# A wide first matmul for 79 of the 128 expert "up" slabs, with the sum of its two halves on VectorE

## The chip, the cores and the metric

The kernel runs on one core of a Trainium2 chip. The metric is the device time of one launch in microseconds (us). The engines named are TensorE (PE, with its weight loads as PEld), VectorE (DVE), ScalarE (ACT), GpSimd (POOL) and SyncE (SP), which here only issues DMAs.

## The reference

A block of a language model runs over 256 tokens of width 1024, all in float32: a mixer (state space and short convolution), PEER (a feed-forward part with 16,384 experts of one neuron each), and then linear attention (HGRN2), a gated FFN, windowed attention and a second gated FFN. The change is in PEER and in two orders of linear attention:

```python
def peer_ffn(n, w_q, sub_keys, expert_u, expert_v):
    q = (t @ w_q).reshape(T, PEER_HEADS, 2, PEER_HALF)
    s = jnp.einsum('thsd,hskd->thsk', q, sub_keys)
    v_half, i_half = lax.top_k(s, PEER_TOPK)                  # 16 best of 128 keys, twice per head
    cand = v_half[:, :, 0, :, None] + v_half[:, :, 1, None, :]
    best, pos = lax.top_k(cand.reshape(...), PEER_TOPK)       # 16 best of the 256 sums
    experts = i1 * PEER_KEYS + i2
    gates = jax.nn.softmax(best)
    act = gelu(x . u[experts]) * gates                        # 128 of the 16384 experts per token
    return sum(act * v[experts])
...
    q, f, i, g = jnp.split(x @ w_in, 4)                       # linear attention (HGRN2)
    o = hgrn2_chunked(q, k, i, logf)
    return (rms_norm(o, out_norm) * silu(g)) @ w_out
```

## The kernel before

All weights pass as 524 slabs of 128x1024 float32, each by one DMA into a ring of four places (`raw`). TensorE multiplies float32 through the faster f32r format, and keeps the accuracy by splitting each operand in a high part and the rest: `split_hi` (ACT, L237, `whi`) and `split_lo` (DVE, L245, `wlo`) do this for a slab, `xhi` and `xlo` hold the two parts of the input x. A product is `whi*xhi + whi*xlo + wlo*xhi`.

PEER computes all 16,384 hidden values: 128 "up" slabs (numbered 0 to 127 here, N_U in the code), each giving one 128x256 tile, then 128 "down" slabs. An up slab by `up` (L273 to L275) is 8 x 3 matmuls of 256 columns, all summed in the first half of one PSUM bank; two banks take turns. ACT then takes the tile out with a Gelu straight from the bank (L1634), and counts it in the semaphore `up_evac`, on which TensorE waits before it writes that bank again: slab k+2 can't begin before the tile of slab k is out. A slab's place in `whi` is free for `split_hi` of slab k+4 when TensorE is through with slab k. SP stores the tile in memory.

Meanwhile DVE finds the experts: sorting work for each head, laid between the `split_lo` of slabs 0 to 62 by a planner (`plan`). It walks the slabs at 2.85 us each, charges 1.25 us for a split that DVE makes itself (POOL makes that of every other slab up to slab 47's step), and fills each step k with units ("half", "pairs", "places", "one_hots", "picked", "numbers") while they fit. In step k DVE makes the low split of slab k+3, then the units of step k. When all is known, six transposes stand in front of slab 59 (COLS_AT), and beside slabs 63 to 126 (E1 = 63, 64 steps) the gates are scattered to a table: in each step DVE makes one-hot rows for four tokens (`one_token`, L1847) and one tile for four (`four_tokens`, L1853), TensorE multiplies them in two pairs, one in the middle of the slab and one after it (L1591), and ACT takes the result out (L1664).

The gated FFNs already use another form, `up_halves` (L294, L298): `xhi` and `xlo` stand side by side in `x2`, so that one matmul of 512 columns takes both with the same weights `whi`, its result filling both halves of a bank, and `wlo*xhi` is added to the second half. That is 8 matmuls of 512 and 8 of 256 columns. It waits for the low split only in its middle. The two halves of the bank must then be added: ACT copies the one (L2523), DVE adds the other from the bank (L2574).

Linear attention runs 16 such `up` slabs over four banks, then 16 slabs by `up_wide` (L334 to L336), which writes four banks in the order 0, 1, 2, 3, the first of which has to wait until each bank is emptied of the earlier slabs. At its end, DVE makes split 15 and then `y(0)`, the low part of the first input (L2433) of the first output slab.

Of the kernel before, what the change touches and what calls it, by code (L numbers as in the profile page):

```python
# [131 lines left out]
def build(nc, t):  # L132
    ctx = ExitStack()
    with ctx:
# [185 lines left out]
        def up_wide(pe, n0, k, bank_free=None, banks_out=None):  # L320
# [4 lines left out]
            for tt in range(TT):  # L325
                x = slice(k * SEQ + tt * P, k * SEQ + (tt + 1) * P)
                for nh in range(2):
                    if bank_free is not None:
                        pe.wait_ge(bank_free, 2 * tt + nh + 1)
                    if banks_out is not None:  # L330
                        pe.wait_ge(up_evac, banks_out[2 * tt + nh])
                    o = bank[2 * tt + nh][:, :]
                    w = slice(q * 1024 + nh * 512, q * 1024 + (nh + 1) * 512)
                    nc.tensor.matmul(o, xhi[:, x], whi[:, w], start=k == 0, stop=False)  # L334
                    nc.tensor.matmul(o, xhi[:, x], wlo[:, w], start=False, stop=False)  # L335
                    last = nc.tensor.matmul(o, xlo[:, x], whi[:, w], start=False, stop=k == KT - 1)  # L336
# [1164 lines left out]
        def plan():  # L1501
# [11 lines left out]
            for k in range(E1):  # L1513
# [5 lines left out]
                spent = max(spent, 2.85 * (k - 1)) + (0.0 if k in by_pool else 1.25)  # L1519
# [27 lines left out]
        def pe_peer(pe):  # L1547
# [19 lines left out]
            up(pe, N_U, U_U, 0, 0, 4, SEQ, x_ready=lo_base(T_WQ, 1))  # L1567
            steps(pe, COLS_AT - 1, 4, lambda i, r: up(pe, N_U + 1, U_U + 1, i, r, 4, SEQ))
# [35 lines left out]
        def act_peer(act, chain):  # L1604
# [36 lines left out]
            steps(act, E1 - 12, 4, step1)  # L1641
            for k in range(E1 - 12, COLS_AT):
# [1467 lines left out]
```

## Time and profile before

| | us |
|---|---|
| median of 3 runs | 1676.4 (1676.38 to 1676.55) |
| profiled execution, its own time | 1676.54 |
| its span, first to last instruction | 1674.8 |
| TensorE busy | 1657.1 (99%) |
| DVE busy | 1309.1 (78%) |
| ACT busy | 1024.4 (61%) |
| granted TensorE clock, mean | 0.998 |

The span is the time between the first and the last instruction of the profile; 1.7 us of the execution lie around it. "Busy" of TensorE counts overlapping matmuls, so the pace of a slab is read from the starts of its instructions.

### The profile page before, as it was taken

Reading aid. Unit: us, or ns where it says so; the run is one execution under the profiler, and the core shown is the slowest. Engines: PE = TensorE matmul, PEld = TensorE weight load, DVE = VectorE, ACT = ScalarE, POOL = GpSimd, SP = SyncE. Lnnn points to the kernel's source line nnn. Section 1 sums busy time; section 2 is a strip of 40 time slices with the busy share of each in tenths; the row PEclk is TensorE's granted clock in tenths of the full one; section 3 lists DMA queues with packets and bytes.
Section 4 is the critical chain, followed back from the end, with each engine's and each line's share of the span. In section 5 each row is a group of like instructions: output and inputs, shape, how many; then the busy total and the mean of one; then the engine's idle time right before and its main releaser. Section 6 shows DMA issues by size and latency. Waiting matters only on the chain.

```text
span 1674.8 us, 34396 instructions
## 1 busy us (share of the span) xinstructions
PE 1657.1 (99%) x10855; PEld 1499.6 (90%) x10855; DVE 1309.1 (78%) x2404; ACT 1024.4 (61%) x1620; POOL 135.5 (8%) x121
## 2 busy tenths in 40 slices
PE   8999999999999999999999999999999999999998
PEld 7999899999999999988888888999888888888886
DVE  7867865899877777777777777899777778978776
ACT  7757555767556666655454554765566557766555
POOL 0035200444000000000000000210000000000000
PEclk9999999999999999999999999999999999999999
DMA  6543464777755555477777877542455554346553
GB/s 214 174 151 104 150 226 143 234 228 226 236 189 173 175 175 177 153 249 241 241 248 252 254 246 243 194 152 88 151 166 196 190 189 155 102 162 197 190 191 113
DMA packets 113614, 315.65 MB, mean 188 GB/s; under 512 B 12832, under 2 KB 44832, under 8 KB 113296
## 3 DMA queue, kind: packets, MB, share of 16 engines
q1 hardware_dynamic: 112032, 310.43, 57.4%
q0 software_dynamic: 1200, 4.07, 0.8%
q8 instruction: 37, 0.61, 0.1%
q10 hardware_dynamic: 320, 0.34, 0.1%
q14 instruction: 25, 0.20, 0.0%
HBM read 296.43 MB, written 18.35 MB: 188 GB/s over the span
## 4 chain that ended last, share of the span: by engine, by line
PE 94%; DVE 3%; ACT 2%; issue 1%; DMA 0%; ACTq 0%; DVEq 0%
PE bank L273 12%; PE bank L274 12%; PE bank L275 12%; PE bank L342 11%; PE bank L343 11%; PE bank L344 11%; PE bank L294 9%; PE bank L298 4%; PE bank L1591 3%; PE bank L2085 2%; PE bank L334 1%; PE bank L336 1%; PE bank L335 1%; DVE wlo L245 1%; PE bank L1287 1%
## 5 line engine op out<-in xcount | busy, mean ns | idle before, releaser
L245 DVE TENSOR_TENSOR wlo<-raw,whi 128x1024 fp32r<-128x1024 f32 x499 | 615.4, 1235 | 120.0 <-ACT whi L237 114.0
L237 ACT ACTIVATE whi<-raw 128x1024 fp32r<-128x1024 f32 x524 | 550.5, 1052 | 19.4 <-PE bank L336 11.4
L273 PE MATMUL bank<-x,whi 128*128 128x256 f32 (+3 forms) x1712 | 499.7, 292 | 0.7 <-DVE x L723 0.3
L275 PE MATMUL bank<-x,wlo 128*128 128x256 f32 (+3 forms) x1712 | 484.2, 283 | 0.0
L274 PE MATMUL bank<-x,whi 128*128 128x256 f32 (+3 forms) x1712 | 483.9, 283 | 0.0
L273 PEld LDWEIGHTS bank<-x,whi 128*128 128x128 f32 x1712 | 326.2, 191 | 3.9 <-issue 1.8
L274 PEld LDWEIGHTS bank<-x,whi 128*128 128x128 f32 x1712 | 326.8, 191 | 0.3
L275 PEld LDWEIGHTS bank<-x,wlo 128*128 128x128 f32 x1712 | 326.1, 190 | 0.0
L342 PE MATMUL bank<-whi,yhi 128*128 128x512 f32 x816 | 319.4, 391 | 1.2 <-DVE ylo L2433 1.1
L343 PE MATMUL bank<-wlo,yhi 128*128 128x512 f32 x816 | 318.1, 390 | 0.0
L344 PE MATMUL bank<-whi,ylo 128*128 128x512 f32 x816 | 317.6, 389 | 0.0
L342 PEld LDWEIGHTS bank<-whi,yhi 128*128 128x128 f32 x816 | 153.3, 188 | 33.1 <-DVE wlo L245 1.3
L344 PEld LDWEIGHTS bank<-whi,ylo 128*128 128x128 f32 x816 | 153.2, 188 | 32.5
L343 PEld LDWEIGHTS bank<-wlo,yhi 128*128 128x128 f32 x816 | 153.4, 188 | 29.7
L294 PE MATMUL bank<-x,whi 128*128 128x512 f32 x704 | 177.6, 392 | 0.8 <-DVE arena L2598 0.7
L1683 ACT ACTIVATE yhi<-h 128x256 fp32r<-128x256 f32 x128 | 53.5, 418 | 170.2 <-PE bank L344 169.6
L294 PEld LDWEIGHTS bank<-x,whi 128*128 128x128 f32 x704 | 129.2, 188 | 27.1 <-DVE arena L2598 1.1
L1634 ACT ACTIVATE h<-bank 128x256 f32<-128x256 f32 x128 | 49.2, 384 | 148.8 <-PE bank L275 148.6
L1892 DVE TENSOR_TENSOR ylo<-h,yhi 128x256 fp32r<-128x256 f32 x128 | 54.5, 425 | 68.2 <-ACT yhi L1683 68.0
L298 PEld LDWEIGHTS bank<-x,wlo 128*128 128x128 f32 x704 | 96.7, 190 | 6.7
L298 PE MATMUL bank<-x,wlo 128*128 128x256 f32 x704 | 100.3, 283 | 0.0
L1847 DVE TENSOR_SCALAR h<-iota,h 128x128 f32<-128x128 f32 x256 | 77.0, 344 | 21.7 <-PE bank L1591 21.7
(354 smaller groups left out, 1777.0 us busy)
## 6 DMA issues: line engine op xcount, KB each, us to landing
raw<-in_stream SPq DMA_DIRECT2D x524, 512.0 KB, 3.6
act_spill<-h SPq DMA_DIRECT2D x124, 128.0 KB, 3.3
h<-act_spill SPq DMA_DIRECT2D x124, 128.0 KB, 3.7
h<-in_x SPq DMA_DIRECT2D x2, 512.0 KB, 5.0
arena<-in_keys POOLq DMA_DIRECT2D x1, 1024.0 KB, 5.9
h_spill<-h SPq DMA_DIRECT2D x1, 1024.0 KB, 6.2
arena<-h_spill POOLq DMA_DIRECT2D x8, 128.0 KB, 3.7
arena<-in_g_final POOLq DMA_DIRECT2D x4, 128.0 KB, 3.7
```

Source lines behind the costliest of these rows:

```text
L237: nc.scalar.activation(whi[:, q * 1024:(q + 1) * 1024], raw[:, q * 1024:(q + 1) * 1024], ACT.Copy).then_inc(hi_ready, 1)
L245: nc.vector.tensor_tensor(wlo[:, q * 1024:(q + 1) * 1024], raw[:, q * 1024:(q + 1) * 1024], whi[:, q * 1024:(q + 1) * 1024].bitcast(F32), ...
L273: nc.tensor.matmul(bank[b][:, 0:T], whi[:, w], xhi[:, x], start=k == 0, stop=False)
L274: nc.tensor.matmul(bank[b][:, 0:T], whi[:, w], xlo[:, x], start=False, stop=False)
L275: last = nc.tensor.matmul(bank[b][:, 0:T], wlo[:, w], xhi[:, x], start=False, stop=k == KT - 1)
L294: return nc.tensor.matmul(bank[b][:, :], whi[:, w], both, start=k == 0, stop=k == KT - 1)
L298: return nc.tensor.matmul(bank[b][:, SEQ:2 * SEQ], wlo[:, w], xhi[:, k * SEQ:(k + 1) * SEQ], start=False, stop=stop, skip_group_check=True)
L342: nc.tensor.matmul(o, yhi[:, y], whi[:, w], start=first, stop=False, skip_group_check=True)
L343: nc.tensor.matmul(o, yhi[:, y], wlo[:, w], start=False, stop=False, skip_group_check=True)
L344: return nc.tensor.matmul(o, ylo[:, y], whi[:, w], start=False, stop=True, skip_group_check=True)
L1847: nc.vector.tensor_scalar(HOT1[:, y % 2 * P:(y % 2 + 1) * P], iota[:, :], c1(I1T), c1(GT_COLS), ALU.is_equal, ALU.mult).then_inc(s("hot_a" ...
L1892: nc.vector.tensor_tensor(ylo[:, yq * SEQ:(yq + 1) * SEQ], PRD[:, yq * SEQ:(yq + 1) * SEQ], yhi[:, yq * SEQ:(yq + 1) * SEQ].bitcast(F32), ...
```

## The change

In PEER, slabs 48 to 126 (H0 = E1 - 15 = 48; 15 slabs ahead of the scatter and the 64 beside it) are multiplied by `up_halves`; slab 127 stays with `up`. ACT, which had one Gelu from the bank, now has a copy of the second half of the bank (`half_out`) and a Gelu in place for the slab before (`half_gelu`). DVE gets one addition per slab (`half_sum`), which alone frees the bank. The planner charges 0.45 us for it. In the scatter loop DVE's low split comes one step later than it did. Stores and reads of the tiles wait for new semaphores. In linear attention the first wide slab takes the banks in the order in which they come free, and `y(0)` stands ahead of split 15. The keys' DMA counts in another semaphore.

```diff
-            for tt in range(TT):
+            for b in sorted(range(4), key=lambda b: banks_out[b] if banks_out else b):
+                tt, nh = b // 2, b % 2
...
+        H0 = E1 - 15
...
-                spent = max(spent, 2.85 * (k - 1)) + (0.0 if k in by_pool else 1.25)
+                spent = max(spent, 2.85 * (k - 1)) + (0.0 if k in by_pool else 1.25) + (0.45 if k > H0 else 0.0)
...
-            steps(pe, COLS_AT - 1, 4, lambda i, r: up(pe, N_U + 1, U_U + 1, i, r, 4, SEQ))
+            if H0:
+                steps(pe, H0 - 1, 4, lambda i, r: up(pe, N_U + 1, U_U + 1, i, r, 4, SEQ))
+            k1 = max(H0, 1)
+            steps(pe, COLS_AT - k1, 4, lambda i, r: up_halves(pe, N_U + k1, U_U + k1, i, r, 4))
...
-                up(pe, N_U + E1, U_U + E1, i, r, 4, SEQ, between=lambda: pair(i, r, 0))
+                up_halves(pe, N_U + E1, U_U + E1, i, r, 4, between=lambda: pair(i, r, 0))
                 pair(i, r, 1)
...
+            def half_out(k0, i, r):
+                q = (k0 + r) % 4
+                act.wait_ge(slabs_done, at(N_U + k0, i, r, 4) + 1 + RING)
+                act.wait_ge(spill_sem(q), rounds(k0, i, r, 4) * 16 + 16)
+                nc.scalar.activation(HR[:, q * SEQ:(q + 1) * SEQ], bank[(U_U + k0 + r) % 2][:, SEQ:2 * SEQ], ACT.Copy)\
+                    .then_inc(s("u_half"), 1)
...
+            def half_gelu(k0, i, r):
+                q = slice((k0 + r) % 4 * SEQ, ((k0 + r) % 4 + 1) * SEQ)
+                act.wait_ge(up_evac, at(U_U + k0, i, r, 4) + 1 + 2)
+                nc.scalar.activation(HR[:, q], HR[:, q], ACT.Gelu).then_inc(s("u_act"), 1)
...
+            def step_halves(k):
+                split_hi(act, N_U + k + AHEAD, 0, 0, 4)
+                half_out(k, 0, 0)
+                if k > H0:
+                    half_gelu(k - 1, 0, 0)
...
+            def half_sum(k0, i, r):
+                q = slice((k0 + r) % 4 * SEQ, ((k0 + r) % 4 + 1) * SEQ)
+                dve.wait_ge(s("u_half"), at(k0 - H0, i, r, 4) + 1)
+                nc.vector.tensor_tensor(HR[:, q], HR[:, q], bank[(U_U + k0 + r) % 2][:, 0:SEQ], ALU.add)\
+                    .then_inc(up_evac, 1)
...
                     split_lo(dve, N_U + k + AHEAD, 0, 0, 4)
+                if k > H0:
+                    half_sum(k - 1, 0, 0)
                 for kind, tt, arg in UNITS_AT[k]:
                     unit(kind, tt, arg)
...
+            def step(k0, i, r):
+                one_token(k0, i, r, 0)
+                one_token(k0, i, r, 1)
+                if k0:
+                    split_lo(dve, N_U + E1 + k0 - 1 + AHEAD, i, r, 4)
+                half_sum(E1 + k0 - 1, i, r)
+                one_token(k0, i, r, 2)
+                one_token(k0, i, r, 3)
+                four_tokens(k0 + 1, i, r)
...
             normed(1, 1)
+            y(0)
             split(15)
-            y(0)
             gated(1)
```

On VectorE, around steps 48 to 50 of PEER, the order before was this (L245 is a low split; L1793 is the last unit of step 48, L1748 to L1754 are "places" in step 49, L1766 and L1775 "one_hots" and "picked" in step 50):

```order
L1793 TENSOR_TENSOR arena<-arena 128x256 [waits dve_self]
L245 TENSOR_TENSOR wlo<-raw,whi 128x1024 [waits hi_ready]
L1748 TENSOR_SCALAR arena<-arena 128x128
L1749 TENSOR_SCALAR arena<-arena 128x128
L1751 CAST arena<-arena 128x256 [waits dve_self]
L1754 CAST arena<-arena 128x256 [waits dve_self]
L245 TENSOR_TENSOR wlo<-raw,whi 128x1024 [waits hi_ready,dve_self]
L1766 TENSOR_TENSOR arena<-arena 128x2048
L1775 TENSOR_TENSOR arena<-arena 128x2048 [waits dve_self]
L245 TENSOR_TENSOR wlo<-raw,whi 128x1024 [waits hi_ready,dve_self]
```

and it is now this (L1868 is `half_sum`, the first one that of slab 48):

```order
L1826 TENSOR_TENSOR arena<-arena 128x256 [waits dve_self]
L245 TENSOR_TENSOR wlo<-raw,whi 128x1024 [waits hi_ready]
L1868 TENSOR_TENSOR h<-h,bank1 128x256 [waits u_half]
L1781 TENSOR_SCALAR arena<-arena 128x128
L1782 TENSOR_SCALAR arena<-arena 128x128
L1784 CAST arena<-arena 128x256 [waits dve_self]
L1787 CAST arena<-arena 128x256 [waits dve_self]
L245 TENSOR_TENSOR wlo<-raw,whi 128x1024 [waits hi_ready,dve_self]
L1868 TENSOR_TENSOR h<-h,bank0 128x256 [waits u_half]
L1799 TENSOR_TENSOR arena<-arena 128x2048
L245 TENSOR_TENSOR wlo<-raw,whi 128x1024 [waits hi_ready,dve_self]
L1868 TENSOR_TENSOR h<-h,bank1 128x256 [waits u_half]
```

The sum of slab k stands in step k+1 behind the low split of slab k+4 and behind all units of step k. "picked" has moved a step on; later "numbers" moves from step 52 to 53, the next "one_hots" from 52 to 54 and "picked" from 53 to 55, where it stands with the last "numbers" and the gates.

On ScalarE, steps 49 and 50 were three lines, a high split, a Gelu from the bank and a high split (L1634):

```order
L237 ACTIVATE whi<-raw 128x1024 [waits slabs_done,raw_ready1]
L1634 ACTIVATE h<-bank0 128x256 [waits act_moved1,slabs_done]
L237 ACTIVATE whi<-raw 128x1024 [waits slabs_done,raw_ready2]
L1634 ACTIVATE h<-bank1 128x256 [waits act_moved2,slabs_done]
L237 ACTIVATE whi<-raw 128x1024 [waits slabs_done,raw_ready3]
```

and now the Gelu of the slab before (L1656), which waits for the sum on DVE through `up_evac`, stands between the copy (L1649) and the next high split:

```order
L237 ACTIVATE whi<-raw 128x1024 [waits slabs_done,raw_ready1]
L1649 ACTIVATE h<-bank0 128x256 [waits act_moved1,slabs_done]
L1656 ACTIVATE h<-h 128x256 [waits up_evac]
L237 ACTIVATE whi<-raw 128x1024 [waits slabs_done,raw_ready2]
L1649 ACTIVATE h<-bank1 128x256 [waits act_moved2,slabs_done]
L1656 ACTIVATE h<-h 128x256 [waits up_evac]
```

On TensorE, in a step of the scatter, the first pair of one-hot products (L1598, before L1591) now follows eight matmuls of 512 columns:

```order
L294 MATMUL bank0<-x2,whi 128x512 [waits up_evac]
L294 MATMUL bank0<-x2,whi 128x512 x7
L1593 ISA
L1595 REGISTER_ALU [waits hot_a]
L1598 MATMUL bank2<-ylo,h 128x128 [waits g_evac,hot_b]
L1593 REGISTER_ALU
L1598 MATMUL bank2<-ylo,h 128x128 [waits hot_a]
L298 MATMUL bank0<-x2,wlo 128x256 [waits lo_ready]
L298 MATMUL bank0<-x2,wlo 128x256 x7
```

It stood behind twelve of 256 columns, and the low split was waited for at the start of the slab; the wait for `lo_ready` now stands in the middle.

## Rows read from the trace of the kernel before

**Rows 1.** The page, busy time by engine (us, share, instructions).
```profile
PE 1657.1 (99%) x10855; PEld 1499.6 (90%) x10855; DVE 1309.1 (78%) x2404; ACT 1024.4 (61%) x1620; POOL 135.5 (8%) x121
```
**Rows 2.** Timeline ahead of the scatter: start us, length us, engine, line, operation [idle before].
```profile
427.49 0.38 ACT L1634 ACTIVATE h<-bank 128x256 f32<-128x256 f32 x1 [1.55 <-PE bank L275]
427.77 1.05 ACT L237 ACTIVATE whi<-raw 128x1024 fp32r<-128x1024 f32 x1
...
453.21 0.82 PE L1575 MATMUL bank<-ident,arena 128*128 128x128 f32 x6
```
**Rows 3.** Chain of waits, one gated FFN step: start us, us, what.
```profile
1238.02 1.81 PE bank L294 x8
1239.83 0.95 PE bank L298 x8
1240.79 1.84 PE bank L294 x8
```
**Rows 4.** Timeline, first and last of 128 groups of one-hot products.
```profile
466.82 0.61 PE L1591 MATMUL bank<-ylo,h 128*128 128x128 f32 x4
...
705.58 0.61 PE L1591 MATMUL bank<-yhi,h 128*128 128x128 f32 x4
```
**Rows 5.** Timeline of POOL and DVE at steps 47 to 49.
```profile
422.20 2.53 POOL L253 TENSOR_TENSOR wlo<-raw,whi 128x1024 fp32r<-128x1024 f32 x1 [3.87 <-DVE wlo L245]
...
429.00 1.22 DVE L245 TENSOR_TENSOR wlo<-raw,whi 128x1024 fp32r<-128x1024 f32 x1
430.14 0.22 DVE L1748 TENSOR_SCALAR arena<-arena 128x128 uint32<-128x128 uint32 x1
```
**Rows 6.** Groups by form: busy us, mean ns, idle before. The FFN's sum from a bank.
```profile
L2574 DVE TENSOR_TENSOR arena<-arena,bank 128x256 f32<-128x256 f32 x44 | 18.5, 420 | 18.0 <-ACT arena L2523 18.0
```
**Rows 7.** Timeline at the first output slab of linear attention.
```profile
1187.52 1.22 DVE L245 TENSOR_TENSOR wlo<-raw,whi 128x1024 fp32r<-128x1024 f32 x1
1187.75 0.47 ACT L2234 ACTIVATE yhi<-bank,arena 128x256 fp32r<-128x256 f32 x1 [0.62 <-PE bank L2135]
...
1188.65 0.48 DVE L2433 SCALAR_TENSOR_TENSOR ylo<-bank,arena,yhi 128x256 fp32r<-128x256 f32 x1
...
1189.28 0.47 PE L342 MATMUL bank<-whi,yhi 128*128 128x512 f32 x1 [1.13 <-DVE ylo L2433]
```
**Rows 8.** Timeline of units on DVE, and of ACT's exponentials, steps 50 to 53.
```profile
432.55 1.22 DVE L1766 TENSOR_TENSOR arena<-arena 128x2048 bf16<-128x2048 bf16 x1
...
436.53 1.28 ACT L1645 ACT_TABLE_LOAD   x1
...
437.34 1.47 DVE L1783 TENSOR_TENSOR arena<-arena 128x1024 bf16<-128x1024 bf16 x3
```
**Rows 9.** Waits between 421 and 466 us: us in total, times, longest.
```profile
DVE wlo L245 <- ACT whi L237: 7.8, 5, 2.3
```
**Rows 10.** Waits between 466 and 706 us, the scatter.
```profile
DVE wlo L245 <- ACT whi L237: 29.7, 64, 0.6
DVE h L1847 <- PE bank L1591: 21.7, 62, 0.4
```
**Rows 11.** Timeline, first wide slab to the second level, and one window (columns: rows 12).
```profile
1106.93 0.47 PE L334 MATMUL bank<-whi,x 128*128 128x512 f32 x1 [0.56 <-ACT arena L2190]
...
1122.09 1.31 DVE L2369 COPY arena<-bank 128x512 f32<-128x512 f32 x2
...
1123.54 3.81 PE L2085 MATMUL bank<-arena 128*128 128x128 f32 x32
...
1113.00:1120.00 7.00, 7.00 (x52) 6.48 (x51) 7.00 (x9) 4.87 (x6) 0.00 (x0) 1.00 0.65 178
```
**Rows 12.** Timeline and windows (PE, PEld, DVE, ACT, POOL busy, clock, DMA), start and end.
```profile
5.18 4.85 PE L835 MATMUL bank<-yhi 128*128 128x512 bf16 x11 [5.18 <-DMA h<-in_x]
...
1666.38 0.39 PE L344 MATMUL bank<-whi,ylo 128*128 128x512 f32 x1
...
1668.80:1669.00 0.20, 0.00 (x0) 0.00 (x0) 0.20 (x2) 0.00 (x0) 0.00 (x0) 0.88 0.00 0
```

More of the change, by code:

```diff
@@ L324, in up_wide @@
             pe.wait_ge(lo_ready, n0 + k + 1)
-            for tt in range(TT):
+            for b in sorted(range(4), key=lambda b: banks_out[b] if banks_out else b):
+                tt, nh = b // 2, b % 2
                 x = slice(k * SEQ + tt * P, k * SEQ + (tt + 1) * P)
[L327 to L336, printed above, removed]
+                if bank_free is not None:
+                    pe.wait_ge(bank_free, b + 1)
+                if banks_out is not None:
+                    pe.wait_ge(up_evac, banks_out[b])
+                o = bank[b][:, :]
+                w = slice(q * 1024 + nh * 512, q * 1024 + (nh + 1) * 512)
+                nc.tensor.matmul(o, xhi[:, x], whi[:, w], start=k == 0, stop=False)
+                nc.tensor.matmul(o, xhi[:, x], wlo[:, w], start=False, stop=False)
+                last = nc.tensor.matmul(o, xlo[:, x], whi[:, w], start=False, stop=k == KT - 1)
             last.then_inc(slabs_done, 1)
@@ L1639, in step1 @@
                 gelu(N_U, U_U, i, r)
-            steps(act, E1 - 12, 4, step1)
-            for k in range(E1 - 12, COLS_AT):
+            def step_halves(k):
[3 more added lines that the diff above has]
+                    half_gelu(k - 1, 0, 0)
+            steps(act, min(H0, E1 - 12), 4, step1)
+            for k in range(min(H0, E1 - 12), COLS_AT):
                 if k == E1 - 10:
@@ L1667, in act_peer @@
             split_hi(act, N_U + E1 + AHEAD, 0, 0, 4)
-            gelu(N_U + E1, U_U + E1, 0, 0)
+            half_out(E1, 0, 0)
+            half_gelu(E1 - 1, 0, 0)
             def step2(i, r):
@@ L1842, in dve_peer, with one_token @@
                     columns()
-            def one_token(i, r, y):
-                n = i * (4 * TPS) + r * TPS + y
+            def one_token(k0, i, r, y):
+                n = i * (4 * TPS) + (k0 + r) * TPS + y
                 dve.wait_ge(s("hot_free"), n - 2 + 1 + TPS)
@@ L1919, in pool_peer @@
             pool.wait_ge(y_lo, 16)
-            pool.dma_start(KEY, t["keys"]).then_inc(s("keys_in"), 16)
+            pool.dma_start(KEY, t["keys"]).then_inc(s("tri"), 16)
             for a in range(TOPK):
@@ L1956, in act_dram, with store @@
                     t["act_spill"][bass.ds(k, 1)].rearrange("a p c -> (a p) c")
-            def put(i, r):
-                sp.wait_ge(up_evac, at(U_U, i, r, 4) + 1 + 2)
-                sp.dma_start(act_dram(i, r), HR[:, r * SEQ:(r + 1) * SEQ]).then_inc(spill_sem(r), 16)
-            def store(i, r):
-                load(sp, N_U + lead, i, r, 4)
-                put(i, r)
-            steps(sp, KEYS - 2 * KEPT, 4, store)
-            for r in range(KEPT):
-                store(KEYS // 4 - 2, r)
+            def store(k0, i, r):
+                load(sp, N_U + lead + k0, i, r, 4)
+                if k0 < H0:
+                    sp.wait_ge(up_evac, at(U_U + k0, i, r, 4) + 1 + 2)
+                else:
+                    sp.wait_ge(s("u_act"), at(k0 - H0, i, r, 4) + 1)
+                q = (k0 + r) % 4
+                sp.dma_start(act_dram(i, r, k0), HR[:, q * SEQ:(q + 1) * SEQ]).then_inc(spill_sem(q), 16)
+            if H0:
+                steps(sp, H0, 4, lambda i, r: store(0, i, r))
+            steps(sp, KEYS - 2 * KEPT - H0, 4, lambda i, r: store(H0, i, r))
+            for k in range(KEYS - 2 * KEPT, KEYS - KEPT):
+                store(k, 0, 0)
             for k in range(KEYS - KEPT, KEYS):
```

43 lines of the change are left out of this document (24 added, 19 removed).

## The prediction

> **What bounds the kernel now.** I read the page's busy times first: TensorE is busy 1657.1 of 1674.8 us, 99% [rows 1]. So time is won by a shorter stream of matmuls alone, and any wait put in front of TensorE is lost in full. Next the timeline ahead of the scatter, for the pace of a slab: the Gelu of slab 49 starts at 427.49 and starts 0.25 us after the slab's last issue slot, so slab 49 ends at 427.24; the transposes behind slab 58 start at 453.21 [rows 2]. That is 25.97 us for 9 slabs, 2.88 us each, without a gap. The wide form is seen in the FFN: 1.81 + 0.95 us, the next slab starting 2.77 us after the first [rows 3]. In the scatter, group 1 of the one-hot products starts at 466.82 and group 128 at 705.58 [rows 4]: 127 halves in 238.76 us, 3.76 us for a step, of which 2.88 are the slab and 0.88 the two pairs. The first group stands 12 matmuls of 0.12 us into slab 63, which therefore begins at 465.4.
>
> **What the wide matmul gives.** 2.88 - 2.77 = 0.11 us per slab, 64 x 0.11 = 7.0 us in the scatter and 15 x 0.11 = 1.6 us ahead of it. The columns are the same (24 x 256 = 8 x 512 + 8 x 256); what goes is the fixed part of eight matmuls, 0.0135 us each. The Trainium skill speaks against this gain (TensorE: Matmul & The Clock Gate, "Wait — 56ns, not 53.3ns?"): a back-to-back matmul costs N/2.4 GHz plus about 2.5 ns. By that, as an estimate from the page, eight matmuls fewer are worth 0.02 us, and all 79 slabs 1.6 us. The rows show five times that per matmul, and I go by the rows.
>
> **The stretch ahead of the scatter.** Here the change adds a wait, and DVE is late for it. The bank of slab k, which slab k+2 needs, was freed by ACT's Gelu right behind slab k. It is now freed by DVE's sum, which stands in step k+1, behind all units of step k and behind a low split. DVE's low split of step 49 starts at 429.00, because step 48 waited for POOL's split (422.20 + 2.53 = 424.73) and then had a "pairs" unit [rows 5]. Nothing in those steps has changed. The low split holds DVE 1.14 us (430.14 - 429.00) [rows 5], and the sum takes 0.42, as the FFN's does [rows 6]: bank free at 430.56. How TensorE restarts from a DVE wait is seen in the first output slab of linear attention: 0.15 us after the 0.48 us that start at 1188.65, with a first matmul 0.08 longer than the usual 0.39 [rows 7], so 0.23 us. Slab 50 would start at 430.8. Its two predecessors in the wide form end at 427.02 (427.24 - 2 x 0.11). TensorE waits **3.8 us** there; before, DVE's lag cost nothing, since only slab 52 needed that low split.
>
> From there DVE, ACT and TensorE run in a ring. After slab k: 0.25 until ACT's copy, 0.28 to issue the next (427.49 to 427.77 [rows 2]), 0.30 for the Gelu of slab k-1, 1.05 for the high split [rows 2], 0.04 hop, 1.14 low split, 0.42 sum, 0.23 restart, 2.77 for slab k+2: 6.48 us for two slabs, 3.24 each against 2.88. Units come on top, 1.25 us for "one_hots", "picked" or "places", 1.9 for "numbers" (three additions in 1.47 and a last one of 0.4) [rows 8]; the exponentials cost ACT a table load of 1.28 us [rows 8] and some 0.4. Walking the steps with these, starts of slabs are (wait in brackets):
>
> slab 51 at 433.8 (0.2), 52 at 437.3 (0.7), 53 at 440.3 (0.2), 54 at 445.4 (2.4, exponentials ahead of the high split of step 53), 55 at 448.8 (0.6), 56 at 451.9 (0.3), 57 at 457.6 (3.0, "picked", "numbers" and gates in step 55: 4.2 us ahead of the sum), 58 at 460.6 (0.2), 59 at 464.1 (none, the transposes fill it), 60 at 467.4 (0.6), 61 at 470.6 (0.4), 62 at 473.9 (0.6), 63 at 477.0 (0.4).
>
> The waits add to 13.3 us with slab 50's 3.8; less the 1.6 of the wide form, slab 63 begins **11.6 us later** than the 465.4 of before. The same walk without sums gives DVE's splits of steps 58 to 62 within 0.1 us of where they are. That DVE has no air here is also in the waits: it stood only 7.8 us, five times, between 421 and 466 us, all behind step 57 [rows 9]. Bounds: nothing, if DVE somehow ran ahead (below); 15 if each hop is 0.2 longer. I take 11.6.
>
> **The scatter.** DVE stood 29.7 us in 64 waits for the high split and 21.7 in 62 for the one-hot products [rows 10], 0.8 us per step. The new sum takes 0.35 to 0.42 of it. Since the low split now asks for a high split made a step earlier, the first wait goes. Order of a step from the start of the second pair: DVE's first token at +0.57, low split +1.08, sum +2.22, third token +2.9 (it waits for the first pair, which comes 0.37 later in the wide slab), fourth done at +3.5; the pair needs it at +3.9. Slack about 0.3 us, so TensorE still sets the pace: **-7.0 us**. If the ring were 0.1 us too long per step, 6.4 us would be lost. At the end of the scatter one more Gelu stands ahead of the first `yhi`, some 0.1 us for TensorE.
>
> **The two orders of linear attention.** TensorE waited 0.56 us for bank 0 at 1106.93; the new order can start 0.7 us sooner. But at the second level product it starts at 1123.54, 0.14 after DVE's copy of 1122.09 + 1.31, and DVE has no idle time on the way there (7.00 of 7 us in 1113 to 1120) [rows 11]. DVE isn't any earlier, so TensorE only waits longer there: 0, with -0.7 as the bound. At the output, `yhi` is there at 1188.22 and `y(0)` ran at 1188.65 because of the split at 1187.52 [rows 7]: ahead of it, TensorE starts at 1188.85 instead of 1189.28, **-0.4 us**. The next late thing is `y(1)`, done at 1191.5, wanted at 1191.6; if that slips it gives back 0.2. The semaphore edit of the keys changes no time.
>
> **TensorE's clock.** The last matmul ends at 1666.77, and the granted clock is 0.88 in the mean of 1668.8 to 1669.0 [rows 12]: it fell from 2.4 to 1.2 GHz 2.2 us after TensorE stopped. The kernel's first eleven matmuls of 512 columns, after 5.2 us of nothing, took 4.85 us, 0.43 each, against 0.227 in the FFN [rows 12, 3]. The longest wait of before inside the work is 1.1 us [rows 7]; the new waits are 3.8, 2.4 and 3.0. A fall costs between 0 and half of 4.85, 2.4 us. I take 1.4 for one fall (slab 50's end is on the ring, so it is not hidden). The Trainium skill agrees that idling brings it (TensorE: Matmul & The Clock Gate, "What's actually happening"): the default is throttled, and activity releases it. Whether waits of 3 us inside a busy stretch do it, no row shows.
>
> **Sum.** The profiled execution took 1676.54, 0.1 above the median of 1676.4. 1676.5 + 11.6 - 7.0 - 0.4 + 0.1 = 1680.8; with one fall of the clock 1682.2.
>
> **Rivals.**
> - *Forecast, with the clock falling at least once*: 1682.2, chance 0.45; two falls 1683.6. Without a fall 1680.8, chance 0.25.
> - *DVE keeps up, and all 79 slabs gain.* The place is slab 50: it decides whether DVE's step 49 reaches its sum before 427.0. For it: the planner charges 0.45 us per step and moves four units later. Against: the step is 3.5 us late already, by steps that the change leaves alone. It gives 79 x 0.11 = 8.7 less 0.4: 1676.5 - 9.1 = 1667.4. Chance 0.11.
> - *The ring is looser than I think*, the big waits stand but the small ones vanish, or part of a wait is caught up: 9.2 instead of 13.3 us of waits, and the wide slab order gives its 0.7: 1676.5 + 7.6 - 7.0 - 0.4 + 0.1 - 0.7 = 1676.1 and up to 1679. Chance 0.12.
> - *The scatter is paced by DVE's tokens*: `one_token` of the fourth token comes too late for the second pair. For it: the slack is 0.3 us out of 3.65, and a Gelu and a sum more in loops with their register work. The gain of 7.0 falls to 0 to 1: 1688. Chance 0.07.
>
> **How the numbers follow.** I call it slower above 1679.8 and faster below 1673.0; 0.2% is about what can be told from no change. Slower holds the two forecasts (0.70), the last rival and a little of the third less what may fall short of 1679.8: 0.72. Faster is the second rival and a little more: 0.12. The same: 0.16. The range of 8 in 10 has to reach the third rival and takes half of the way to the last: 1675 to 1687; the forecast's own is 1679.5 to 1685.
>
> **What would show it.** Right: TensorE waits for DVE's sum ahead of slabs 50, 54 and 57 by 2 to 4 us each, the sum L1868 is the releaser, and the first one-hot product starts at about 478.8 (or 480 with a fall) instead of 466.82. Its 127 halves then take 232 us instead of 238.8. PEclk shows a stretch below 1.0 around 430. `y(0)` is 0.4 us earlier, and the second level product is not earlier relative to the first wide slab's end by more than 0.1. Wrong: waits ahead of the scatter under 5 us in sum, or a scatter step of 3.76 us or more.

## The result, and the profile after

The changed kernel took 1688.15 us in the median of 4 runs (1687.2 to 1689.3), the kernel before 1676.47 (1676.38 to 1676.56, 4 runs): a ratio of 1.007, with a 95% interval of 1.0053 to 1.0087. It is slower, as forecast, but by 11.7 us instead of 5.8, and 1.15 us above the upper end of the range. The runs of before lie within 0.2 us of each other, those of the changed kernel within 2.1. The profiled execution took 1687.20, its span is 1685.4.

The page's busy times, which answer to [rows 1]:

```profile
PE 1657.3 (98%) x10223; PEld 1470.3 (87%) x10223; DVE 1334.9 (79%) x2483; ACT 1045.1 (62%) x1699; POOL 135.4 (8%) x121
```

TensorE has 632 matmuls fewer, 79 slabs times eight, and is busy 0.2 us longer. The busy time fell by what the wide form saves and rose by what slower clocks and restarts cost; the kernel of the first experiment below, with the wide form beside the scatter alone and none of those waits, is busy 1653.5 us.

The timeline of TensorE ahead of the scatter (start us, length us, line, tile and shape, in brackets the idle time before it and its releaser), slabs 50 to 51, 52, 54 and 57 to 58, then the transposes, slabs 60 to 63 and the first one-hot products. A long phase has eight matmuls of 512 columns (L294), a short one eight of 256 (L298):

```profile
426.10 1.11 PE L298 MATMUL bank<-x,wlo 128*128 128x256 f32 x8
430.53 2.94 PE L294 MATMUL bank<-x,whi 128*128 128x512 f32 x8 [3.31 <-DVE h L1868]
433.27 1.86 PE L298 MATMUL bank<-x,wlo 128*128 128x256 f32 x8
434.97 1.98 PE L294 MATMUL bank<-x,whi 128*128 128x512 f32 x8
...
438.52 2.12 PE L294 MATMUL bank<-x,whi 128*128 128x512 f32 x8 [0.62 <-DVE h L1868]
...
446.74 2.11 PE L294 MATMUL bank<-x,whi 128*128 128x512 f32 x8 [2.10 <-DVE h L1868]
...
459.01 3.58 PE L294 MATMUL bank<-x,whi 128*128 128x512 f32 x8 [2.70 <-DVE h L1868]
...
463.38 2.00 PE L294 MATMUL bank<-x,whi 128*128 128x512 f32 x8
...
466.17 0.82 PE L1582 MATMUL bank<-ident,arena 128*128 128x128 f32 x6
...
470.21 2.08 PE L294 MATMUL bank<-x,whi 128*128 128x512 f32 x8 [0.23 <-DVE h L1868]
...
479.73 2.11 PE L294 MATMUL bank<-x,whi 128*128 128x512 f32 x8
481.68 0.61 PE L1598 MATMUL bank<-ylo,h 128*128 128x128 f32 x4
```

The three long waits, ahead of slabs 50, 54 and 57, stand where the forecast put them, and DVE's sum (L1868) ends each. What made each of them long is taken up in the experiments. The transposes, at 453.21 before [rows 2], are at 466.17. The second thing to see is the length of two slabs: slab 50 runs from 430.53 to 434.97, 4.44 us, and slab 57 from 459.01 to 463.38, 4.37 us, where slab 58 takes 2.79. Their matmuls run slower, and the windows (PE, PEld, DVE, ACT, POOL busy, then granted clock, DMA share, GB/s) say why:

```profile
430.00:435.00 5.00, 4.47 (x17) 3.92 (x18) 4.23 (x9) 1.37 (x2) 0.00 (x0) 0.66 0.40 133
...
445.00:450.00 5.00, 3.06 (x16) 2.52 (x16) 4.74 (x9) 3.18 (x6) 0.00 (x0) 1.00 0.47 167
...
455.00:460.00 5.00, 2.30 (x12) 1.90 (x11) 3.66 (x8) 1.48 (x3) 0.00 (x0) 0.88 0.37 129
460.00:465.00 5.00, 5.00 (x23) 4.16 (x22) 1.56 (x2) 1.69 (x4) 0.00 (x0) 0.77 0.39 131
```

The granted clock fell from 2.4 to 1.2 GHz for a part of slab 50 and a part of slab 57, at waits of 3.31 and 2.70 us. Finer windows put the first fall at 431.5 us, 1.0 us after slab 50 had started, and the second at 458.8, 0.2 us before slab 57 started. The clock did not fall at the wait of 2.10 us ahead of slab 54, whose window shows 1.00.

Where DVE is late, its timeline shows for slab 50:

```profile
428.58 0.42 DVE L1826 TENSOR_TENSOR arena<-arena 128x256 f32<-128x256 f32 x1
428.92 1.22 DVE L245 TENSOR_TENSOR wlo<-raw,whi 128x1024 fp32r<-128x1024 f32 x1
430.06 0.41 DVE L1868 TENSOR_TENSOR h<-h,bank 128x256 f32<-128x256 f32 x1
```

The low split starts at 428.92 as it started at 429.00 before [rows 5], right behind its units, and only then comes the sum that frees the bank: free at 430.47, and TensorE starts at 430.53.

In the scatter the chain of waits (start us, us, what) is one step:

```profile
561.42 1.85 PE bank L294 x8
563.27 0.44 PE bank L1598 x4
563.71 0.95 PE bank L298 x8
564.66 0.45 PE bank L1598 x4
565.11 1.85 PE bank L294 x8
```

It is 3.69 us against 3.76 before, all of it TensorE; some steps take up to 3.72. The first and the last of the 128 groups, as [rows 4], and the one before the last:

```profile
481.68 0.61 PE L1598 MATMUL bank<-ylo,h 128*128 128x128 f32 x4
...
714.85 0.61 PE L1598 MATMUL bank<-yhi,h 128*128 128x128 f32 x4
...
716.25 0.61 PE L1598 MATMUL bank<-yhi,h 128*128 128x128 f32 x4
```

234.57 us for 127 halves; it was 238.76. The difference of 4.19 makes the gain look too large, because the halves of a step are no longer alike (1.39 and 2.30 us, where each had 1.88), and from the first to the last group there is one short half more than there are long ones. Over whole steps it is 714.85 - 481.68 = 233.17 us for 63 of them, 3.70 each against 3.76: 0.06 us a step, 3.8 us for 64. And the first output slab of linear attention, as [rows 7], waits 0.74 instead of 1.13:

```profile
1199.69 0.47 PE L342 MATMUL bank<-whi,yhi 128*128 128x512 f32 x1 [0.74 <-DVE ylo L2485]
```

The ledger of the two profiled executions, in shifts of the same instruction, starts from two more rows. Slab 63 and the down stage begin in the kernel before at:

```profile
465.38 0.28 PE L273 MATMUL bank<-x,whi 128*128 128x256 f32 x1
...
708.90 0.46 PE L342 MATMUL bank<-whi,yhi 128*128 128x512 f32 x1
```

and in the changed kernel (slab 63 is shown above) at:

```profile
719.69 0.47 PE L342 MATMUL bank<-whi,yhi 128*128 128x512 f32 x1
```

Slab 63 starts 14.35 us later (479.73 - 465.38). The down stage starts 10.79 later (719.69 - 708.90). The stretch from the last one-hot product to it takes 3.44 us instead of 3.32, +0.12, so the scatter gave 3.68. Linear attention's first output slab stands at +10.41 (1199.69 - 1189.28), so -0.38 for the order; and the last matmul at 1677.06 instead of 1666.38, +10.68. The last 0.27 appears behind linear attention, where two waits of the FFNs' slabs for DVE sum to 1.0 us instead of 0.7 (0.36 and 0.64 instead of 0.35 and 0.34); why the second grew is open. The profiled execution is the fastest of the four.

### The profile page after: what moved, and what is told of

It is laid out like the page before. It is cut to its first block, busy times and chain, and to the rows that moved or that the text cites. A ratio compares the mean times of both kernels' runs of the same rounds, so it can differ in the third digit from the quotient of the medians.

```text
span 1685.4 us, 33407 instructions
## 1 busy us (share of the span) xinstructions
PE 1657.3 (98%) x10223; PEld 1470.3 (87%) x10223; DVE 1334.9 (79%) x2483; ACT 1045.1 (62%) x1699; POOL 135.4 (8%) x121
## 4 chain that ended last, share of the span: by engine, by line
PE 91%; DVE 5%; ACT 2%; issue 1%; DMA 0%; POOL 0%; ACTq 0%; DVEq 0%
PE bank L294 17%; PE bank L342 11%; PE bank L343 11%; PE bank L344 11%; PE bank L298 8%; PE bank L273 7%; PE bank L275 7%; PE bank L274 7%; PE bank L1598 3%; PE bank L2137 2%; DVE wlo L245 1%; ACT whi L237 1%; PE bank L334 1%; PE bank L336 1%; PE bank L335 1%
## 5 line engine op out<-in xcount | busy, mean ns | idle before, releaser
L245 DVE TENSOR_TENSOR wlo<-raw,whi 128x1024 fp32r<-128x1024 f32 x499 | 614.9, 1234 | 100.1 <-ACT whi L237 94.3
L294 PE MATMUL bank<-x,whi 128*128 128x512 f32 x1336 | 345.2, 399 | 10.9 <-DVE h L1868 9.7
L273 PE MATMUL bank<-x,whi 128*128 128x256 f32 (+3 forms) x1080 | 310.7, 288 | 0.7 <-DVE x L723 0.3
L275 PE MATMUL bank<-x,wlo 128*128 128x256 f32 (+3 forms) x1080 | 305.8, 283 | 0.0
L274 PE MATMUL bank<-x,whi 128*128 128x256 f32 (+3 forms) x1080 | 305.6, 283 | 0.0
L294 PEld LDWEIGHTS bank<-x,whi 128*128 128x128 f32 x1336 | 243.6, 189 | 60.4 <-DVE h L1868 7.6
L273 PEld LDWEIGHTS bank<-x,whi 128*128 128x128 f32 x1080 | 205.8, 191 | 3.9 <-issue 1.8
L274 PEld LDWEIGHTS bank<-x,whi 128*128 128x128 f32 x1080 | 206.0, 191 | 0.3
L275 PEld LDWEIGHTS bank<-x,wlo 128*128 128x128 f32 x1080 | 205.8, 191 | 0.0
L298 PE MATMUL bank<-x,wlo 128*128 128x256 f32 x1336 | 194.1, 286 | 0.0
L298 PEld LDWEIGHTS bank<-x,wlo 128*128 128x128 f32 x1336 | 178.9, 191 | 8.1
L1649 ACT ACTIVATE h<-bank 128x256 f32<-128x256 f32 x79 | 30.2, 383 | 95.2 <-PE bank L298 95.2
```

The costliest lines, as they stand in the source:

```text
L245: nc.vector.tensor_tensor(wlo[:, q * 1024:(q + 1) * 1024], raw[:, q * 1024:(q + 1) * 1024], whi[:, q * 1024:(q + 1) * 1024].bitcast(F32), ...
L273: nc.tensor.matmul(bank[b][:, 0:T], whi[:, w], xhi[:, x], start=k == 0, stop=False)
L274: nc.tensor.matmul(bank[b][:, 0:T], whi[:, w], xlo[:, x], start=False, stop=False)
L275: last = nc.tensor.matmul(bank[b][:, 0:T], wlo[:, w], xhi[:, x], start=False, stop=k == KT - 1)
L294: return nc.tensor.matmul(bank[b][:, :], whi[:, w], both, start=k == 0, stop=k == KT - 1)
L298: return nc.tensor.matmul(bank[b][:, SEQ:2 * SEQ], wlo[:, w], xhi[:, k * SEQ:(k + 1) * SEQ], start=False, stop=stop, skip_group_check=True)
```

## The experiments

The kernels are measured beside runs of before on the same chip (medians 1676.38 to 1676.48). The diffs are against the changed kernel unless the text says otherwise, and show the edit's main lines; line numbers in the rows are those of the run's own kernel, so that the one-hot products can stand at L1598 or L1601 and the sum at L1868, L1871 or L1876.

**Only the scatter in the wide form.** The 15 slabs ahead of it stay as they were.

```diff
-        H0 = E1 - 15
+        H0 = E1 - 0
...
-                step_halves(k)
+                if k < H0:
+                    split_hi(act, N_U + k + AHEAD, 0, 0, 4)
+                    gelu(N_U + k, U_U + k, 0, 0)
+                else:
+                    step_halves(k)
```

> The changed kernel with the wide form beside the scatter alone (64 slabs, none ahead of it); both orders of linear attention kept. Theory (the waits for DVE's sum ahead of the scatter and the clock falling in them cost some 14.5 us, the scatter gains 0.07 us a step): no wait of TensorE for the sum, granted clock 1.00 between 420 and 480 us, first one-hot product at about 466.9 us, step 3.69 us, 1676.5 - 4.3 - 0.4 + 0.1 = 1671.9 us, runs within 0.3. Rival A (the loss is in the scatter or behind it, or spread): 1680 or more. Rival B (0.11 us per slab, lost only in that one execution): step 3.65, 1669.3 us.

Measured: 1672.8 us (1672.33 to 1673.64, 11 runs), ratio 0.998 (0.9971 to 0.9989). Its first and last groups of one-hot products:

```profile
466.99 0.60 PE L1601 MATMUL bank<-ylo,h 128*128 128x128 f32 x4
...
701.58 0.61 PE L1601 MATMUL bank<-yhi,h 128*128 128x128 f32 x4
```

234.59 us for the 127 halves, as in the changed kernel to 0.02, and the first starts within 0.2 us of where it did before: its slab begins 0.23 sooner (465.15), and ahead of it stand eight long matmuls with 1.84 us instead of twelve short ones with 1.44. The scatter's part of the change is a gain of some 3.8 us: the span is 4.2 below that of before, and 0.4 of it belongs to the order of `y(0)` (below). The whole loss sits in the 15 slabs ahead of the scatter: 1688.15 - 1672.8 = 15.4 us. The median is 0.9 above what was expected. In the profiled run, one of the longer ones, 2.9 us of the 1673.54 lie outside the span of 1670.6, where another run has 1.9 (1672.63 with 1670.7). What makes the difference outside the span I can't say.

**The long waits filled with matmuls.** The changed kernel, with matmuls of 512 columns that write an unused bank ahead of the three slabs.

```diff
-            steps(pe, COLS_AT - k1, 4, lambda i, r: up_halves(pe, N_U + k1, U_U + k1, i, r, 4))
+            for k in range(k1, COLS_AT):
+                for _ in range({50: 14, 54: 8, 57: 11}.get(k, 0)):
+                    nc.tensor.matmul(bank[6][:, :], xhi[:, 0:P], xhi[:, 0:512], start=True, stop=True)
+                up_halves(pe, N_U + k, U_U + k, 0, 0, 4)
```

> The changed kernel with extra matmuls of 512 columns into an unused bank ahead of slabs 50 (14), 54 (8) and 57 (11), which TensorE can run while it waits for DVE's sum; the output is unchanged. Theory (the clock falls to 1.2 GHz in the two long waits, and each fall costs 1.6 us): granted clock 1.00 from 425 to 465 us, slabs 50 and 57 last 2.8 instead of 4.4 and 4.3 us, 3.1 us less than the profiled 1687.2: 1684.1 us, runs within 0.5 of each other where the changed kernel's spread over 2.1. Rival (the slow slabs are hidden behind DVE's lag, and cost nothing): 1687 to 1688. Rival (the extra matmuls delay slab 50): above 1688.

Measured: 1684.29 us (1684.15 to 1684.47, 4 runs), ratio 1.0047 (1.0031 to 1.0062). The timeline at slabs 50 and 57:

```profile
427.05 3.36 PE L1577 MATMUL bank<-x 128*128 128x512 f32 x14
430.62 2.06 PE L294 MATMUL bank<-x,whi 128*128 128x512 f32 x8 [0.20 <-DVE h L1871]
432.51 1.11 PE L298 MATMUL bank<-x,wlo 128*128 128x256 f32 x8
...
454.75 2.68 PE L1577 MATMUL bank<-x 128*128 128x512 f32 x11
457.62 2.08 PE L294 MATMUL bank<-x,whi 128*128 128x512 f32 x8 [0.19 <-DVE h L1871]
459.54 1.11 PE L298 MATMUL bank<-x,wlo 128*128 128x256 f32 x8
```

Slab 50 starts within 0.1 us of where it starts in the changed kernel, so the bank comes free no sooner: the wait is there, filled. But its long phase takes 1.89 us (432.51 - 430.62) and not 2.74, and slab 57 starts 1.39 us sooner. The clock is 1.00 in every window of 5 us from 425 to 475. In medians that is 3.9 us less, in the profiled executions 2.7, and slab 63 starts at 476.86 instead of 479.73. The runs lie within 0.3 us of each other instead of 2.1. So the falls of the clock are a cost of their own, and they are also what makes the changed kernel's times spread.

**The sum ahead of the split.** All 15 slabs stay in the wide form; DVE takes the two in the other order.

```diff
             for k in range(E1):
+                if k > H0:
+                    half_sum(k - 1, 0, 0)
                 if not pool_splits(k):
...
                     split_lo(dve, N_U + k + AHEAD, 0, 0, 4)
-                if k > H0:
-                    half_sum(k - 1, 0, 0)
```

> The changed kernel with one edit: ahead of the scatter DVE's sum of slab k-1 stands before the low split of slab k+3. Theory (the ring copy, Gelu, high split, low split, sum paces TensorE between the big waits, and lag of DVE's units makes the big ones): the small waits of 0.2 to 0.7 us go, waits remain of about 2.6 us at slab 50, 1.7 at 55, 2.9 at 57; 1677.8 us, or 1679.4 with one fall of the clock and 1681 with two. Rival (only the lag of the units matters, not the place of the sum): within 1 us of the changed kernel, 1687 to 1688.

Measured: 1679.41 us (1678.36 to 1682.94, 10 runs), ratio 1.0019 (1.0009 to 1.0028). Its waits and the clock of two windows:

```profile
PE bank L294 <- DVE h L1868: 6.4, 3, 2.7
```

```profile
430.00:435.00 5.00, 5.00 (x21) 4.29 (x20) 4.60 (x9) 1.84 (x4) 0.00 (x0) 0.66 0.37 134
...
455.00:460.00 5.00, 4.80 (x14) 4.09 (x15) 2.71 (x4) 1.36 (x2) 0.00 (x0) 0.50 0.40 134
```

And its timeline at slabs 50, 57, 58 and what follows it:

```profile
429.36 2.76 PE L294 MATMUL bank<-x,whi 128*128 128x512 f32 x8 [2.19 <-DVE h L1868]
...
455.20 3.75 PE L294 MATMUL bank<-x,whi 128*128 128x512 f32 x8 [2.67 <-DVE h L1868]
...
460.46 2.43 PE L294 MATMUL bank<-x,whi 128*128 128x512 f32 x8
...
463.69 0.82 PE L1582 MATMUL bank<-ident,arena 128*128 128x128 f32 x6
```

Three waits of 6.4 us in sum are left of eight with 9.7: the ring of ACT's copy, high split, low split, sum and restart no longer sets the pace of every slab, and slabs follow each other in 2.79 us between the waits. In medians the kernel is 8.7 us faster than the changed one, but not all of that is the ring. Slab 63 starts at 475.52 in the profiled run, 4.5 us of which are its two falls (1.6 and 2.8, below); without them it would be 471.0, 5.8 sooner than in the kernel with the waits filled (476.86). So some 5.8 us are the ring. The other 2.9 I put down to falls that cost the median run less here; only one run of the ten has a trace, so that part is argued and not shown. What is left is DVE's own lateness: 2.19 us ahead of slab 50, 1.49 ahead of 55, 2.67 ahead of 57. The profiled run still has both falls, and the second is longer than either of the changed kernel's profile: slabs 57 and 58 take 5.26 and 3.23 us, 2.8 more than 2.87 + 2.79. There the clock was down already in the wait, 2.1 us after slab 56's last matmul had been issued:

```profile
454.60:455.00 0.40, 0.00 (x0) 0.00 (x0) 0.40 (x3) 0.00 (x0) 0.00 (x0) 0.50 0.05 20
```

It stayed down for 6.8 us, where each fall of the changed kernel lasted 3.4. The profiled run is the slowest of the ten, 4.6 us above the fastest, with the same instructions. The median equals the 1679.4 that was expected with one fall, though how many falls that run had isn't known; the profiled run, with two, is 1.9 above the 1681 expected for that.

**Seven slabs ahead of the scatter instead of 15**, once in the changed kernel's order of DVE and once with the sum first. Both have `H0 = E1 - 7` and the branch of the first experiment.

> The wide form begins at slab 56 instead of 48, and DVE keeps the changed kernel's order: the low split first, then the sum. The only difference from the seven-ahead kernel with the sum first (1671.97) is that order. Theory (each slab's bank hangs on the ring ACT copy, high split, low split, sum): a wait of about 1.0 us ahead of slab 58 and 0.3 to 0.6 ahead of 60 to 62, 2.4 to 2.8 in sum, all short, so no fall of the clock: 1671.97 + 2.6 = 1674.6. Rival one, the changed kernel's lateness comes only from the units of steps 47 to 55, and the order matters only there: no wait left, 1672.0. Rival two, the wide form ahead of the scatter brings the long waits and the falls wherever it begins: 1676 and more.

> Wide form for slabs 56 to 126 (7 ahead of the scatter, behind the last units), and in the steps ahead of the scatter DVE's sum of slab k-1 stands before the low split of slab k+3. Theory: the sum is then done 1.14 us sooner, the ring takes some 5.3 us for two slabs, less than TensorE's 5.6, so TensorE never waits there; 7 slabs gain 0.09 us each: 0.5 below scatter_only, 1671.4 us. Rival (any wide slab ahead of the scatter costs, whatever the order, as ACT has one more instruction between two high splits): above scatter_only by 1 us or more.

Measured: 1674.55 us (1674.23 to 1674.86, 11 runs), ratio 0.9989 (0.998 to 0.9998) with the split first, and 1671.97 us (1671.9 to 1672.36, 8 runs), ratio 0.9974 (0.9964 to 0.9985) with the sum first. With the split first the timeline has these waits:

```profile
450.83 2.06 PE L294 MATMUL bank<-x,whi 128*128 128x512 f32 x8 [0.72 <-DVE h L1876]
457.60 2.08 PE L294 MATMUL bank<-x,whi 128*128 128x512 f32 x8 [0.30 <-DVE h L1876]
464.04 2.06 PE L294 MATMUL bank<-x,whi 128*128 128x512 f32 x8 [0.29 <-DVE h L1876]
```

With the sum first there is none for a sum of PEER in the whole execution, and slab 63 starts at 464.84 instead of 467.06. The difference of 2.6 us is the ring alone, without a late unit and without a fall of the clock. It is measured for slabs whose units were long done, so the ring costs time without them, and the first rival, that the order matters only beside units, falls. In the scatter, where the sum also stands behind the low split, TensorE has no wait for it, so it is not a cost in every place. The version with the sum first beats the kernel before by 4.4 us (beside 1676.38 on its chip) and the changed one by 16.2; it is 0.6 us above what was expected of it.

**Seven `pairs` units left out.** The changed kernel, with the seven `pairs` of steps 41 to 48 replaced by two small fills each; the best pairs of those heads aren't found.

```diff
                 for kind, tt, arg in UNITS_AT[k]:
+                    if kind == "pairs" and k >= 41:
+                        q16 = slice((tt * PH + arg) * TOPK, (tt * PH + arg + 1) * TOPK)
+                        chain.link(nc.vector.memset(BEST[:, q16], 1.0))
+                        chain.link(nc.vector.memset(POS[:, q16], 0.0))
+                        continue
                     unit(kind, tt, arg)
```

> The changed kernel, with the seven 'pairs' units of steps 41 to 48 left out (the best 16 of the pairs of heads 1 to 7 of the second 128 tokens are replaced by constants, so that part isn't computed). Theory (slab 50 waits because DVE is 3.5 us late by units): the wait ahead of slab 50 falls from 3.3 to about 0.6 us, those ahead of 54 and 57 stay at 2.1 and 2.7, the clock stays at 1.00 around 430 us and may fall once around 459: 1680.8 us, or 1682.4 with that fall. Rival (the wait at slab 50 is a matter of the order copy, split, sum, not of the lag): the wait stays at 2 us or more.

Measured: 1682.56 us (1682.12 to 1682.96, 4 runs), ratio 1.0037 (1.0022 to 1.0051). The timeline at slabs 50, 54 and 57:

```profile
427.27 2.11 PE L294 MATMUL bank<-x,whi 128*128 128x512 f32 x8 [0.22 <-DVE h L1868]
...
441.93 2.12 PE L294 MATMUL bank<-x,whi 128*128 128x512 f32 x8 [1.97 <-DVE h L1868]
...
454.21 3.29 PE L294 MATMUL bank<-x,whi 128*128 128x512 f32 x8 [2.70 <-DVE h L1868]
```

The wait ahead of slab 50 goes from 3.31 to 0.22 and with it goes one of the two falls (the clock is 1.00 from 430 to 435 us): 5.6 us in medians, 4.7 in the profiled executions, which is 3.1 of the wait and 1.6 of the fall. The waits ahead of 54 and 57 stay. So slab 50's long wait has a cause of its own: the units that DVE was behind with already, which before had cost nothing.

**No table loads.** ACT's two exponentials of step 53 become copies, so the gates aren't exponentials, and no table is loaded there.

```diff
-                    nc.scalar.activation(GATE, GATE, ACT.Exp).then_inc(s("gate_e"), 1)
+                    nc.scalar.activation(GATE, GATE, ACT.Copy).then_inc(s("gate_e"), 1)
-                    nc.scalar.activation(LBE, LBE, ACT.Exp).then_inc(s("lb_e"), 1)
+                    nc.scalar.activation(LBE, LBE, ACT.Copy).then_inc(s("lb_e"), 1)
```

> The changed kernel with ACT's two exponentials of step 53 replaced by copies of the same shape, so the gates aren't exponentials, and no activation table is loaded there (two loads of 1.28 us). Theory (the ring of step 53 is as long as ACT's work ahead of the high split): the first load goes from slab 54's wait, 2.1 becomes 0.8, and nothing behind gives it back: 1688.15 - 1.3 = 1686.9; the second load stands beside DVE's units and gives nothing. Rival one: both loads count, 1685.6. Rival two: slab 57's wait hangs on work of DVE that doesn't depend on ACT and takes it all back, 1688.1.

Measured: 1685.24 us (1683.82 to 1686.28, 4 runs), ratio 1.005 (1.0035 to 1.0065). Its timeline at slabs 50, 51, 54 and 57:

```profile
430.56 3.78 PE L294 MATMUL bank<-x,whi 128*128 128x512 f32 x8 [3.32 <-DVE h L1868]
...
435.86 2.10 PE L294 MATMUL bank<-x,whi 128*128 128x512 f32 x8
...
446.23 2.14 PE L294 MATMUL bank<-x,whi 128*128 128x512 f32 x8 [0.66 <-DVE h L1868]
...
458.52 2.53 PE L294 MATMUL bank<-x,whi 128*128 128x512 f32 x8 [2.70 <-DVE h L1868]
```

Slab 54's wait goes from 2.10 to 0.66 us and slab 57's stays at 2.70, which the theory expected. The time fell by 2.9 and not 1.3. I don't read that as a second load that counts: both profiled executions have two falls of the clock, and a fall isn't always the same size. Here slab 50 takes 5.30 us (435.86 - 430.56), with the same instructions as in the changed kernel, where it took 4.44; the clock was down for 6.8 us, from 429.2 on. With the falls taken out of both traces, slab 63 starts some 1.5 us sooner, which is what slab 54's wait lost. On the time in medians the run is inconclusive; on the wait it isn't. No run takes slab 57's wait away. Its cause is read from the changed kernel's trace alone: DVE is busy with the units of step 55 ("picked", "numbers" and the gates) until 457.32, and only then makes the low split and, at 458.45, the sum.

**The two orders of linear attention, each alone in the kernel before.** The wide slab takes its banks in the order in which they come free (`for b in sorted(range(4), key=...)` instead of 0 to 3); and `y(0)` ahead of the split:

```diff
-            split(15)
             y(0)
+            split(15)
```

> The kernel before with one edit: the first wide slab of linear attention takes the banks in the order in which they come free. Theory (DVE paces the levels behind it, so the earlier start is waited away): TensorE's wait at the wide slab goes, a wait of 0.5 us for DVE's copy comes at the second level product, 1676.5 us, within 0.1 of before. Rival (the start is kept): 1675.8.

> The kernel before with one edit: in linear attention's output DVE makes y(0) ahead of split 15. Theory: TensorE's wait for it shrinks from 1.1 to 0.7 us and nothing gives it back: 1676.1 us. Rival (y(1), which comes later by one low split, is then late and takes it back): 1676.5.

Measured: 1676.44 us for the bank order (1676.26 to 1676.61, 11 runs), ratio 1.0 (0.9991 to 1.0009), and 1676.11 us for `y(0)` (1675.94 to 1676.26, 11 runs), ratio 0.9998 (0.9989 to 1.0007), beside 1676.48 of before. The runs of `y(0)` and of before don't all lie apart, and the interval holds 1, but the trace has the gain: TensorE waits 0.74 us there and not 1.13, and starts at 1188.83 instead of 1189.28. For the bank order, in its own trace (to be held against [rows 11]):

```profile
1106.16 0.40 PE L334 MATMUL bank<-whi,x 128*128 128x512 f32 x1
...
1123.50 3.81 PE L2085 MATMUL bank<-arena 128*128 128x128 f32 x32 [0.50 <-DVE arena L2369]
```

The first wide slab starts 0.77 us sooner (1106.16 instead of 1106.93), and the second level product, at 1123.54 before, starts at 1123.50. The wait has moved from the first to the second of these places, and hangs on DVE there.

## Why the prediction was wrong in size and right in direction

- **Direction and place: right.** TensorE is busy 99% of its time and a new wait in front of it is lost in full. Leaving out the 15 slabs ahead of the scatter takes away all of the loss.
- **The walk of the waits: right.** Forecast for the start of slab 63 without a fall 477.0; the kernel with the waits filled, where the clock doesn't fall, has it at 476.86, the changed kernel at 479.73. Waits by start times were 3.8, 2.4 and 3.0 in the forecast; the trace names 3.31, 2.10 and 2.70 as idle, and by start times they are 3.48 (430.53 - 427.05, the end of slab 49's issue, 426.10 + 0.95), 2.26 and 2.86. Each is 0.1 to 0.3 shorter than forecast. The others were short and repeated, as walked: slabs 60 to 63 follow each other in 3.08 to 3.25 us, where the ring gave 3.24.
- **The ring: right**, and shown by the sum taken first: 2.6 us in seven slabs, and some 5.8 of the 8.7 in the 15.
- **Clock: one of the two steps that failed.** I wrote "I take 1.4 for one fall" and gave one fall the forecast. There were two, 4.44 - 2.84 = 1.6 and 4.37 - 2.87 = 1.5 in the profiled execution (the lengths of the same slabs with the waits filled, 432.51 + 0.95 - 430.62 and 459.54 + 0.95 - 457.62). At slab 63 they are 2.9 (479.73 - 476.86), in medians 3.9. The size for one was near; my upper bound of 2.4 was passed by the two long falls, 2.5 (slab 50 without the table loads, 5.30 - 2.84) and 2.8 (the sum first). What was wrong is the count: all three long waits of the walk were longer than the 2.2 us behind which the clock had fallen at the end of the kernel [rows 12], so one fall was not the likeliest case. The Trainium skill (TensorE: Matmul & The Clock Gate, "What's actually happening") says that the default state is throttled and that activity releases it. The trace agrees in that the clock fell only where TensorE had idled, 3.31 and 2.70 us, and shows that this happens inside a busy stretch too. The step misses by 1.5 us in the profiled execution and 2.5 in medians.
- **Scatter: the other step that failed, and the larger one.** "2.88 - 2.77 = 0.11 us per slab ... 7.0 us" is 3.76 - 3.70 = 0.06 per step, and 3.7 us in all (from the start of slab 63 to the last one-hot product). The mechanism was right and the term mis-sized, by 3.3 us. My 1.81 us for the long phase was a phase that follows matmuls of 512 columns. The third row of [rows 3] shows 1.84 for one that follows eight of 256; in the scatter it follows four of 128 and takes 1.85. And the two pairs take 0.44 and 0.45 where I had 0.44 for each. With the third row the sum would have been 2.88 - 2.79 = 0.09 and 5.8 us: nearer, and still 2.1 too much. The Trainium skill's figure of about 2.5 ns of fixed time per matmul (TensorE: Matmul & The Clock Gate, "Wait — 56ns, not 53.3ns?") would have given 1.3 us for the scatter, as an estimate from the page. The runs show 3.7, 0.007 us per matmul saved, so the page's figure is too small here, and yet missed by less (2.4) than the row that I went by.
- **DVE's room in the scatter: right**; no wait of TensorE there.
- **Order of `y(0)`, -0.4: right** (-0.37 alone). **Bank order, 0: right** (0.0 alone). **End of the scatter, +0.1: right** (0.12).
- The two errors have the same sign. In the profiled execution they add to 4.8 of the 5.0 us between the forecast's shifts and the measured one (5.7 and 10.68 us). In medians they are 5.8 of the 5.95 between 1682.2 and 1688.15.
- Of the rivals, "DVE keeps up" and "the ring is looser" are out. "The scatter is paced by DVE's tokens" was priced at 1688 and so comes nearest to 1688.15, but by chance: the scatter did gain, and TensorE has no wait in it. "Two falls" was the right mechanism, priced at 1683.6: with 3.7 for the scatter instead of 7.0 and 2.9 for the falls it gives 1680.8 + 3.3 + 2.9 = 1687.0, beside the profiled 1687.20. The forecast's own range ended at 1685, and the stated one at 1687, half of the way to the last rival; neither left room for the two unknown sizes to be wrong together.

## What to carry to other kernels

When an engine has no idle time, count first which engine now gives it its buffers back, and where in that engine's queue the release stands: in this kernel a release of 0.4 us behind a split of 1.1 us cost some 5.8 us in fifteen slabs, without the slower clock, where the wide form saved 3.7 us in sixty-four. A wait in front of TensorE has two prices, its length and the slower slab that follows if the clock falls; filling the wait with matmuls that do nothing tells the two apart in one run. A duration should be taken from a row whose neighbours are the same as where it will stand. And a gain per step is read over whole steps: where the change moves work from one half of a step to the other, an interval that begins in one half and ends in the other counts that too.

## What the runs showed of the hardware

- The granted clock fell in the middle of a dense stream. Idle times of 2.10 us (the changed kernel, slab 54) and 1.97 us (without the pairs) left it at 1.00; 2.19 us (the sum first, slab 50), 2.67 to 2.70 us (four kernels, slab 57) and 3.31 us did not. The length of the wait alone doesn't say when it falls: in the sum first it was down 2.1 us after the last matmul had been issued (454.5, slab 57), in the changed kernel only 1.0 us after TensorE had started again (431.5, slab 50).
- The falls came in two sizes. Five lasted 3.4 us and made the slab behind the wait and the next 1.5 to 1.6 us longer together; two lasted 6.8 us (the sum first at slab 57, without the table loads at slab 50) and made them 2.5 and 2.8 us longer. Which came where was not the same in two executions of the same instructions: the runs of the kernels with two such waits spread over 2.1 to 4.6 us, those of the kernel with the waits filled over 0.3.
- A long phase of eight matmuls of 512 columns takes 1.84 to 1.85 us behind matmuls of 256 or 128 columns, and 1.81 behind matmuls of 512.
- The restart behind a DVE instruction varies. At slab 50 DVE's sum ends at 430.47 and TensorE starts at 430.53, 0.06 us later; at slab 57 it ends at 458.86 and TensorE starts at 459.01, 0.15 later, as in [rows 7].
